# A four-layer transformer kernel on one core: 56 modulation weight blocks beside the softmax units instead of the projections

## What is computed

```python
mod = silu(c) @ ada_w[l] + ada_b[l]          # 1024 x 6144 weights, two vectors (latent, context)
sh1, sc1, g1, sh2, sc2, g2 = split(mod, 6)
h = x * (1 + sc1) + sh1
p = concat([hc, h]) @ w_in                    # the projection
s = einsum(q, k) * 64 ** -0.5
p = softmax(s)                                # layer 1: p[0] - lam * p[1]
o = einsum(p, v)
x = layer_norm(ALPHA * x + g1 * (concat([o, pool or conv]) @ w_out))
x = layer_norm(ALPHA * x + g2 * swiglu(x * (1 + sc2) + sh2))
```

## Time and profile before

| | us |
|---|---|
| median of 3 runs (lowest, highest) | 3386.14 (3385.05, 3392.02) |
| the profiled execution's own time | 3385.06 |
| its span in the profile | 3383.3 |
| PE busy in it | 3147.6 (93%) |
| PEld busy | 2717.5 (80%) |
| DVE busy | 2099.1 (62%) |
| ACT busy | 1258.3 (37%) |

### The profile page before, as it was taken

How to read it: one execution, slowest core, us unless ns; L and a number is a source line. 1 busy time by engine, 2 the same in 40 slices (tenths; PEclk the granted TensorE clock), 3 DMA queues, 4 the chain that set the end, 5 groups by cost and what they waited for, 6 DMA issues and landing times.

```text
span 3383.3 us, 52710 instructions
## 1 busy us (share of the span) xinstructions
PE 3147.6 (93%) x20288; PEld 2717.5 (80%) x20288; DVE 2099.1 (62%) x3752; ACT 1258.3 (37%) x1920; POOL 105.9 (3%) x135
## 2 busy tenths in 40 slices
PE   6978998999979999698999999999799999999998
PEld 2548998986759978587999999887588899999886
DVE  1376556553466530578976666784559895666686
ACT  1144445431244421231444444432441344444433
POOL 0020000000000000013000000000003000000000
PEclk8999999999989999799999999999899999999999
DMA  7703543547215533033566666674234466665664
GB/s 283 270 7 113 186 168 127 185 142 261 75 50 179 185 132 116 32 126 127 216 243 223 206 204 205 226 243 139 78 120 142 173 230 229 206 225 205 216 236 137
DMA packets 190526, 580.70 MB, mean 172 GB/s; under 512 B 16769, under 2 KB 61825, under 8 KB 185505
## 3 DMA queue, kind: packets, MB, share of 16 engines
q1 hardware_dynamic: 185120, 541.04, 47.1%
q10 hardware_dynamic: 4608, 33.56, 2.4%
q0 software_dynamic: 640, 4.00, 0.3%
HBM read 543.92 MB, written 34.60 MB: 171 GB/s over the span
## 4 chain that ended last, share of the span: by engine, by line
PE 82%; DVE 10%; ACT 3%; issue 1%; DMA 1%; POOL 0%; ACTq 0%; DVEq 0%; SPq 0%; POOLq 0%
PE ps L955 27%; PE ps L1001 26%; PE ps L827 5%; PE ps L782 4%; PE ps L945 3%; PE ps L1232 3%; PE ps L1209 2%; PE ps L830 2%; DVE w_split L2010 1%; PE ps L919 1%; ACT arena L1503 1%; PE ps L985 1%; DVE arena L1780 1%; PE ps L721 1%; PE ps L904 1%
## 5 line engine op out<-in xcount | busy, mean ns | idle before, releaser
L2010 DVE TENSOR_TENSOR w_split<-ring,w_split 128x1024 fp32r<-128x1024 f32 (+1 forms) x707 | 865.4, 1226 | 596.5 <-ACT w_split L1566 595.9
L955 PE MATMUL ps<-x_split,w_split 128*128 128x256 f32 x8352 | 1058.2, 285 | 31.1 <-DVE w_split L2010 17.4
L955 PEld LDWEIGHTS ps<-x_split,w_split 128*128 128x128 f32 x8352 | 1039.3, 193 | 53.4 <-issue 19.6
L1566 ACT ACTIVATE w_split<-ring 128x1024 fp32r<-128x1024 f32 (+1 forms) x707 | 746.6, 1058 | 734.0 <-PE ps L1001 437.6
L1001 PE MATMUL ps<-w_split,h_split 128*128 128x512 f32 x3864 | 914.0, 390 | 3.5 <-DVE w_split L2010 3.5
L1001 PEld LDWEIGHTS ps<-w_split,h_split 128*128 128x128 f32 x3864 | 712.7, 188 | 144.2 <-issue 3.9
L1640 ACT ACTIVATE arena<-ps 128x256 f32<-128x256 f32 (+1 forms) x256 | 98.2, 384 | 497.1 <-PE ps L955 412.6
L827 PE MATMUL ps<-arena,ring 128*128 128x512 f32 (+1 forms) x416 | 155.8, 529 | 11.3 <-DVE arena L2382 6.1
L827 PEld LDWEIGHTS ps<-arena,ring 128*128 128x128 f32 x416 | 81.3, 198 | 75.9 <-issue 69.1
L1209 PE MATMUL ps<-x,ring 128*128 128x256 f32 x608 | 137.2, 382 | 0.0
L782 PE MATMUL ps<-x,ring 128*128 128x256 f32 (+1 forms) x608 | 133.9, 383 | 3.5 <-ACT x L1537 3.5
(11 more groups left out here) (276 smaller groups left out, 2547.7 us busy)
## 6 DMA issues: line engine op xcount, KB each, us to landing
ring<-in_peer_u SPq DMA_DIRECT2D x256, 512.0 KB, 3.3
ring<-in_peer_v SPq DMA_DIRECT2D x256, 512.0 KB, 4.2
ring<-in_ffn_in SPq DMA_DIRECT2D x132, 512.0 KB, 3.2
ring<-in_ada SPq DMA_DIRECT2D x96, 512.0 KB, 6.1
ring<-in_ffn_out SPq DMA_DIRECT2D x66, 512.0 KB, 3.2
spread_rows<-arena ACTq DMA_DIRECT2D x32, 1024.0 KB, 4.0
arena<-spread_rows SPq DMA_DIRECT2D x20, 1536.0 KB, 8.5
ring<-in_pq SPq DMA_DIRECT2D x32, 512.0 KB, 3.3
```

The source lines that it names most:

```text
L955: last = mm(dst, w_split[:, w, wp, at:at + P], rhs[rp], start=(first and i == 0), stop=(final and i == 2), skip_group_check=shared)
L1566: f(w_split[0:rows, w, 0, :], ring[0:rows, slot, :], ACT.Copy).then_inc(w_high, 1)
L2010: v.tensor_tensor(w_split[0:rows, w, 1, :], ring[0:rows, slot, :], w_split[0:rows, w, 0, :].bitcast(F32), ALU.subtract).then_inc(w_low, 1)
```

## The change

32 of the 80 blocks that stood in the projections move beside the first 22 units of layer 0's softmax stage, and 24 beside the first 10 of layer 1's. The projection of layer 0 keeps 16 blocks (2 after each of 8 products), that of layer 1 keeps 8 (1 after each of 8 products). `ADA_BESIDE` says how many blocks go beside each unit. In PE's loop they stand after `scores(i + 2)` and before `heads(i - 1)`; a piece that ended with unit j is copied by ACT in its turn j+1 and turned by PE and biased by DVE in their turns j+2.

The sums of the moved pieces take bank 7 (one of them bank 5). To free it, the outputs of two successive units now lie in two quarters of bank 6. So `heads(i)` on PE waits until ACT has copied out unit i-1, where it waited for unit i-2, and ACT's loop has `heads(i - 2)` ahead of `turned(i - 1)`, where it stood behind; this order is that of all four softmax stages.

```diff
-ADA_AFTER = {0: [4] * 8 + [5, 5, 6, 0], 1: [2] * 16 + [0] * 6}
+ADA_AFTER = {0: [2] * 8 + [0] * 4, 1: [1] * 8 + [0] * 14}
-BIASED_AT = {0: {1: 2, 3: 3, 5: 4, 7: 5}, 1: {0: 8, 3: 9, 7: 10, 11: 11}}
+BIASED_AT = {0: {3: 2, 7: 3}, 1: {3: 8}}
+ADA_BESIDE = {0: [2, 2, 2, 2, 0, 0] * 4, 1: [3, 2, 3] + [2] * 4 + [3, 2, 3] + [0] * 2}
+ADA_BESIDE_FIRST = {l: ADA_FIRST[l] + sum(ADA_AFTER[l]) for l in (0, 1)}
+def piece_beside(l, i):
+    if l > 1 or i < 0 or not ADA_BESIDE[l][i]:
+        return None
+    end = ADA_BESIDE_FIRST[l] + sum(ADA_BESIDE[l][:i + 1])
+    return end // KD - 1 if end % KD == 0 else None
...
         def ada_bank(l, n):
-            return (6 if (l, n) >= (1, 2) else 2) + n % 2
+            if beside(l, n):
+                return 5 if (l, n) == (1, 4) else 7
+            return 6 if (l, n) == (1, 2) else 2 + n % 2
...
                 if k == 0:
-                    pe.wait_ge(ada_out, 6 * l + n - 1)
+                    pe.wait_ge(ada_out, 6 * l + n - (0 if (0, 4) <= (l, n) <= (1, 1) else 1))
...
-                    if base + i >= 2:
-                        pe.wait_ge(o_out, base + i - 1)
+                    if base + i:
+                        pe.wait_ge(o_out, base + i)
...
-                            last = mm(single[rows, i % 2, 0:P], u["v"](c, half),
+                            last = mm(ps[rows, 6, (i % 2) * P:(i % 2 + 1) * P], u["v"](c, half),
...
                     if i + 2 < n:
                         scores(i + 2)
+                    piece = piece_beside(l, i - 2)
+                    if piece is not None:
+                        ada_turn(piece // 6, piece % 6)
+                    if l < 2:
+                        at = ADA_BESIDE_FIRST[l] + sum(ADA_BESIDE[l][:i])
+                        for m in range(at, at + ADA_BESIDE[l][i]):
+                            place.steps(pe, 1, 1, lambda _, par, b: (wait_filled(b[0]), ada_block(m // (6 * KD), m // KD % 6, m % KD, b[0])))
                     if i:
                         heads(i - 1)
                     turn(i)
...
                     if i + 1 < n:
                         exps(i + 1)
+                    if i >= 2:
+                        heads(i - 2)
                     if i:
                         turned(i - 1)
-                    if i >= 2:
-                        heads(i - 2)
+                    piece = piece_beside(l, i - 1)
+                    if piece is not None:
+                        keep_ada(piece // 6, piece % 6, first_block(f"attend{l}") + sum(ADA_BESIDE[l][:i]))
+                if n > 1:
+                    heads(n - 2)
                 turned(n - 1)
-                heads(n - 2)
                 heads(n - 1)
...
                     rotate(l, len(ROPE[0]) - 1)
-                    biased(1, 0)
-                    biased(1, 1)
...
                     if i and not units[i - 1]["diff"]:
                         turned(i - 1)
+                    piece = piece_beside(l, i - 2)
+                    if piece is not None:
+                        biased(piece // 6, piece % 6)
```

More of the change, by code:

```diff
@@ L173, in project_weights, with beside_weights @@
     return blocks
-ADA_AFTER = {0: [4] * 8 + [5, 5, 6, 0], 1: [2] * 16 + [0] * 6}
-ADA_FIRST = {0: 2 * KD, 1: 8 * KD}
-BIASED_AT = {0: {1: 2, 3: 3, 5: 4, 7: 5}, 1: {0: 8, 3: 9, 7: 10, 11: 11}}
+def beside_weights(l):
+    runs, at = [], ADA_BESIDE_FIRST[l]
+    for n in ADA_BESIDE[l]:
+        for _ in range(n):
+            runs.append((f"attend{l}", f"ada{at // (6 * KD)}", 1, at % (6 * KD)))
+            at += 1
+    return runs
+ADA_AFTER = {0: [2] * 8 + [0] * 4, 1: [1] * 8 + [0] * 14}
+ADA_FIRST = {0: 2 * KD, 1: 8 * KD}
+BIASED_AT = {0: {3: 2, 7: 3}, 1: {3: 8}}
[6 more added lines that the diff above has]
+    return end // KD - 1 if end % KD == 0 else None
 def product_block(l, n):
@@ L190, in pieces_after @@
     return range(*done)
-WEIGHTS = [("ada0", "ada0", 2 * KD, 0)] + project_weights(0, "ab_in", 12) + [
-           ("out00", "ab_out", 8), ("hidden00", "ffn0", 0), ("out01", "ab_out", 8), ("hidden01", "ffn0", 0)] + project_weights(1, "cd_in", 22) + [("out11", "cd_out", 8), ("hidden11", "ffn1", 0),
+WEIGHTS = [("ada0", "ada0", 2 * KD, 0)] + project_weights(0, "ab_in", 12) + beside_weights(0) + [
+           ("out00", "ab_out", 8), ("hidden00", "ffn0", 0), ("out01", "ab_out", 8), ("hidden01", "ffn0", 0)] + project_weights(1, "cd_in", 22) + beside_weights(1) + [("out11", "cd_out", 8), ("hidden11", "ffn1", 0),
            ("project2", "ml_in", 26), ("project2", "kv0", 4), ("out21", "ml_out", 8), ("hidden2", "peer0", 0),
@@ L455, in ada_bank, with beside @@
         def ada_bank(l, n):
-            return (6 if (l, n) >= (1, 2) else 2) + n % 2
+            if beside(l, n):
+                return 5 if (l, n) == (1, 4) else 7
+            return 6 if (l, n) == (1, 2) else 2 + n % 2
+        def beside(l, n):
+            return (0, 4) <= (l, n) <= (1, 1) or (l, n) >= (1, 3)
         def ada_sum(l, n):
@@ L1518, in heads @@
                     act.wait_ge(o_ready, base + i + 1)
-                    f(units[i]["out"], single[:, i % 2, 0:P], ACT.Copy).then_inc(o_out, 1)
+                    f(units[i]["out"], ps[:, 6, (i % 2) * P:(i % 2 + 1) * P], ACT.Copy).then_inc(o_out, 1)
                 n = len(units)
```

## The result

| | before | after |
|---|---|---|
| median (lowest, highest), us | 3387.76 (3385.05, 3392.02), 4 runs | 3357.09 (3355.79, 3360.90), 4 runs |
| own time of the profiled execution | 3385.06 | 3355.84 |
| its span | 3383.3 | 3354.1 |

The changed kernel takes 0.991 of the time before (95% interval 0.9893 to 0.9927), 30.7 us less by the medians; the profiled executions differ by 29.2 us. The prediction was 3364 us, that is 21.2 us under the profiled execution before, with a range of 3354 to 3375 us.

A forecast was written before the change was run, and what follows sets the result against it. PE was taken to bound the projections, an ACT-PE ring each softmax unit. -31.6 + 5.4 + 0.8 + 3.8 + 0.4 = -21.2 us against 3385.06 us gave 3364 us, range 3354 to 3375 us.

The forecast's parts named there:

- Projection 0: Layer 0's projection: 32 blocks, their groups, three turnings, the modulation weights' wait and a slow tile leave, 18.8 us off.
- The prices of blocks and turnings: PE in the projections: 0.43 us for each block, 0.14 us for a group, 0.47 us for a turning.
- Projection 1: Layer 1's projection: 24 blocks, eight groups of two and three turnings leave PE, 12.8 us off.
- ACT's copy in the ring: Softmax units: output copy ahead of L1514 lengthens the ACT-PE cycle setting each unit, 0.17 us in 32 units, 5.4 us.
- The blocks' spill: Softmax units: blocks exceeding PE's gap before `heads`, in six layer 1 units; 0.8 us, ends 0 and 1.5.
- The starts at 1.2 GHz: First three units of both softmax stages: blocks run at half clock, 3.8 us added, upper end 10.6 us.
- the rival of the clock that comes back at once: Softmax starts: blocks restore the clock, so starts cost nothing or gain a little; 3359 us, chance 0.14.
- Softmax 1: Layer 1's softmax stage, first scores to first mean of its heads: predicted 4.8 us longer, 2.5 us of it clock.
- The waits of DVE and SP: Softmax stages: DVE's bias waits for PE's turning 7 times, 0.4 us; SP's later fetches of blocks and output weights, 0.
- The rival of late weights: Softmax units: waiting for weights before `heads`, 0.5 us in half of 26 units, 6.5 us; 3370 us, chance 0.05.
- that of the small gap: PE's gap in softmax units: starting a group costs 0.4 us, 26 groups add 10 us; 3374 us, chance 0.10.
- The slower rival: Clock stays at 1.2 GHz through a stage's units, PE bounds them, 34 us more in layer 1; 3398 us, chance 0.04.

The follow-up runs named there:

- run 1: The kernel before with only the shared bank and ACT's new order, no block moved: 3389.46 us, ratio to before 1.0005.
- run 2: The changed kernel with ACT's output copy of unit i-2 ahead of the exponentials of unit i+1: 3351.58 us, ratio to before 0.9889; timed again, 3353.32 us.
- run 3: The changed kernel with one piece of each layer (8 blocks each) left in the projection, so the first softmax units have no blocks: 3368.66 us, ratio 0.994.
- run 4: The kernel of run 1 with matmuls nobody reads, shaped like the blocks, in the first three units of layers 0 and 1: 3394.78 us, ratio 1.0013.
- run 8: Run 2 with five blocks in PE's wait at the start of layer 1's stage only, layer 0's blocks as in the changed kernel: 3351.78 us, ratio 0.9896.
- run 5: The changed kernel with ACT's old order of copies, the bank still shared: 3358.55 us, ratio to before 0.9916.
- run 6: Run 2 with five blocks in PE's wait for each stage's first exponentials and one or two beside the next units: 3352.92 us, ratio 0.9899.

## Why the prediction was right, and where it was off

What leaves the projections and what comes into the stages held in mechanism, sign and place; the gain was 8.0 us larger than the sum, by the profiled executions. Of that, 4.4 us are what the projections gave beyond their prices, 3.5 us what softmax 1 didn't cost. Step by step:

- **Projection 0, 18.8 us predicted, 21.6 measured.** The prices of blocks and turnings held: two blocks take 1.00 us in the changed kernel too. The wait for modulation weights and the slow tile behind it are gone as forecast. Left out were 0.4 us of wait for the projection's own weights, some 0.5 us at the stage's end, where I had put the last turning's cost at nothing, and 1.0 us at the first tile, which took 9.8 us before and 8.8 us now at a low clock and is chance (the changed kernel's second profile has 9.8 us there too).
- **Projection 1, 12.8 predicted, 14.4 measured.** Missing was what a group of blocks costs its neighbours. Two places show it. Before, a rotation behind blocks took 0.53 us (840.30 to 840.83), and the tile at 840.83 handed over to blocks after 6.96 us:

```profile
840.30 0.70 PE L850 MATMUL ps<-arena,consts 128*128 128x256 f32 x2
840.83 7.03 PE L827 MATMUL ps<-arena,ring 128*128 128x512 f32 x16
847.79 1.07 PE L721 MATMUL ps<-ring,cond_wide 128*32 128x256 f32 x16
```

  In the changed kernel, with no blocks beside them, the rotation took 0.43 us and the tile handed over after 6.87 us:

```profile
812.99 0.59 PE L877 MATMUL ps<-arena,consts 128*128 128x256 f32 x2
813.42 7.03 PE L854 MATMUL ps<-arena,ring 128*128 128x512 f32 x16
820.29 0.59 PE L877 MATMUL ps<-arena,consts 128*128 128x256 f32 x2
```

  Eight groups that are gone altogether make 8 x 0.19 = 1.5 us, which is the gap; three more in projection 0 make 0.6 us.
- **ACT's copy in the ring, 5.4 us.** Right in size for a unit (0.17 us in latent units and in layer 1, runs 1 and 2) and in cause (run 2 removes it), but not in number. In layer 0 I had counted 21 units; 17 got longer (2.69 to 2.86, 3.11 to 3.28, 4.20 to 4.37 us), the first four didn't, so it was 2.9 us there instead of 3.6. In those four ACT isn't the bound. DVE is: its division L1915 takes 1.28 us while POOL works, where it takes 0.35 us with POOL idle (L1879 before, at 196.09), and `heads` waits for DVE's half of the copy, L1923:

```profile
165.64 1.28 DVE L1915 TENSOR_SCALAR arena<-arena,cols 128x256 f32<-128x256 f32 x1
165.65 1.13 POOL L655 TENSOR_TENSOR arena<-arena 128x562 f32<-128x562 f32 x1
...
166.84 0.41 DVE L1923 COPY arena<-ps 128x256 f32<-128x256 f32 x1
...
167.36 0.66 PE L946 MATMUL ps<-arena 128*64 128x128 f32 x8 [0.77 <-DVE arena L1923]
```

  The copy's 0.17 us is the one cost of the change that needn't be there.
- **The blocks' spill, 0.8 us between 0 and 1.5.** Layer 1's units measure 4.02 and 4.12 us for 3.85 us, together 1.0 us over the stage, between the two readings and nearer to PE's row. The Trainium skill ("Trainium Kernel Development and Optimization", Performance Expectations) prefers the weight loads' row to the matmuls' for judging how close a kernel is to roofline. Carried over to the room in a gap, as I did, that would have had 0 here; PE's modelled row was the better guide to the room in this one. In context units I had called a pair a fit. They take 2.86 us, the old 2.69 plus 0.17; PE's own work is nearly as long, as run 2 shows, where they fall to 2.81 us and no further.
- **The starts at 1.2 GHz, 3.8 us.** This is the term that was mis-sized most: measured, it is near 0. Turn by turn from the first scores, layer 0's first turning came 1.0 us later than before, and the fourth at 18.24 us against 18.22 us. Layer 1's first came 2.1 us later and its third 0.3 us later.

  In layer 0 it isn't the clock that gave the blocks' time back. The sixth turning comes 24.4 to 24.5 us after the first scores in eleven of the thirteen profiles, with blocks and without, with the clock low for 6.8, 10.2 or 13.7 us, and with any of ACT's three orders. DVE beside POOL sets the pace there, as the rows above show, and PE had time for the blocks beside it. Only where the clock was low for over 20 us (runs 1 and 3) did the sixth turning come later, at 26.6 us.

  The length of the low stretch does follow the blocks in layer 0. With at least two beside each of the first four units it was 6.8 us in all eight profiles (the changed kernel three times, run 2 twice, run 8, run 5, and run 4 with its filler in three units). Without blocks it was 10.2, 13.7, 23.9 and 27.3 us (before twice, runs 1 and 3), and 10.2 us in run 6, whose units behind the first had one block each. Run 4 shows that it is PE's work and not the moved weights. The Trainium skill's rule that activity releases the throttle ("TensorE: Matmul & The Clock Gate", What's actually happening) agrees with these lengths.

  In layer 1 the low stretch was 3.4 us in six profiles with blocks (the changed kernel three times, run 2 twice, run 5), but also in run 3 without; with the full projection ahead it was 10.2, 10.2 and 6.8 us without blocks and 6.8 us with run 4's filler. So there the lengths go with the emptier projection ahead at least as well as with the blocks, and the cause of the earlier return stays open.

  I had named the rival of the clock that comes back at once and given it 0.14. Its price for this term came true, but not by its mechanism in layer 0, and not shown in layer 1; that part of the gain is luck.
- **Softmax 1, 4.8 predicted, 1.3 measured.** Of the difference of 3.5 us, some 2.3 us is the clock term above; the rest is the stage's end, which had a low clock in the first profile before and not in the one of the changed kernel. In the second profile before, without that, the stage took 52.3 us, and the change costs 2.5 us.
- **The waits of DVE and SP, 0.4 us and 0.** No unit with a bias is longer than its neighbours in layer 0, and PE waited for no weights there, nor in layer 1 at 0.90 of the queues' time. The rival of late weights and that of the small gap are out. The slower rival is out too: at the start of layer 1's stage the clock was back by about the first turning. What that rival describes, units that PE sets at 1.2 GHz, did appear in runs 1 and 3 (3.78 us a unit), where no blocks stood.

The range held. What the clock gave by chance nearly cancels in the total: 1.0 us at the first tile and some 1.2 us at the end of softmax 1 for the changed kernel, 2.5 us between softmax 0 and projection 1 against it.

## What to carry to other kernels

Work that depends on nothing should go where the bounding engine waits for others, and its room is read from one repeated unit: which instruction releases the next round, and how much of the gap before it is free. What was put ahead of that releasing instruction cost its time in each unit, as the 128-column copy did here for 0.17 us (recorded as 0.28 us long, with its successor starting before its end); the same copy in front of the instruction that waits anyway was free. Where another engine set the unit, as DVE did beside POOL in layer 0's first units, neither the copy nor the blocks cost anything. And count what a group of small instructions costs the ones beside it, since a whole group that is removed gives more than its own length.

## What the runs showed of the hardware

The length for which TensorE stays at 1.2 GHz after a pause isn't a constant of the kernel. At the start of layer 0's softmax stage, with the same instructions for PE, it was 10.2 and 13.7 us in two executions of the kernel before, and 23.9 us in run 1, whose PE work differs only in a wait and in where the outputs lie; PE was busy 20.2 of 25 us there and the clock stayed down. With two blocks or more, or as many matmuls that nobody reads, in each of the first three units it was 6.8 us in eight profiles of eight. Low stretches elsewhere differ between executions of one kernel too: the work between the two layers, which no run changes, took 492.5 to 496.5 us, longer where the clock was low for longer.
